# Two-layer diffusion backbone on one core: the attention projection cut into 512-column chunks and moved between layer norm, states and retention, the residual spilled to DRAM, retention without its centring and cross-decay steps

## The reference

```python
p_lat = u_lat @ w_in_l                       # u = modulated RMS norm of h
kA, vA, kB, vB, qA, qB, gF, gB, pool, glu = split(p_lat)
# A: differential attention, 4 heads, rotary on q and k
# B: retention in chunks of 128 tokens, forward and backward
scores = einsum('bhncd,bhnmd->bhncm', q, k) * dmat          # dmat = gamma ** distance
y = einsum('bhncm,bhnme->bhnce', scores, v)
cross_decay = exp(lg[:, None] * (j + 1.0))
y = y + einsum('bhncd,nbhde->bhnce', q, s_prev) * cross_decay[...]
# head layer norm: subtract the mean over a head's 64 channels, divide by the deviation
yn = (y - mu) * lax.rsqrt(var + 1e-6)
yB = silu(gF) * yn_forward + silu(gB) * yn_backward
# C: pooling windows, D: gated convolution, layer norm, silu, 256x256 product
h = h + gm * rms_norm(concat(yA, yB, yC, yD) @ w_out)
h = h + gf * rms_norm(swiglu(modulate(rms_norm(h))))
```

## Time and profile before

| | |
|---|---|
| median of three runs | 3718.29 us |
| the profiled execution | 3710.92 us, its span 3709.1 us |
| PE busy | 3221.3 us, 87% |
| DVE busy | 1846.1 us, 50% |
| ACT busy | 1045.0 us, 28% |
| mean granted TensorE clock | 0.881 |

### The profile page before, as it was taken

One profiled execution on the slowest core, in us unless ns is written; L12 is line 12 of the kernel. 1 busy time (PEld: TensorE's weight loads), 2 busy tenths in 40 slices (PEclk: granted clock), 3 DMA queues, 4 the chain that ended last, 5 costly groups with the idle time before them and its releaser, 6 DMA issues.

```text
span 3709.1 us, 45803 instructions
## 1 busy us (share of the span) xinstructions
PE 3221.3 (87%) x17774; PEld 1859.2 (50%) x17774; DVE 1846.1 (50%) x2565; ACT 1045.0 (28%) x1514; POOL 301.9 (8%) x208
## 2 busy tenths in 40 slices
PE   6798778777889999999999489679787899999997
PEld 6344544566454665555545234445666444444443
DVE  1794745788447211222225595746776364122235
ACT  2311213444344111111113311214444353111122
POOL 2400000000121000000002230000000210000001
PEclk8999669566889999999999699778666999999998
DMA  4110010011112321111111100011111222111112
GB/s 182 48 41 17 6 36 35 35 45 45 50 53 89 115 91 63 40 36 44 40 51 63 56 35 35 6 42 46 57 57 40 80 90 103 51 50 47 51 57 102
DMA packets 59451, 206.87 MB, mean 56 GB/s; under 512 B 7360, under 2 KB 8384, under 8 KB 59328
## 3 DMA queue, kind: packets, MB, share of 16 engines
q1 hardware_dynamic: 58176, 199.89, 15.1%
q10 hardware_dynamic: 1152, 5.24, 0.4%
HBM read 200.91 MB, written 4.19 MB: 55 GB/s over the span
## 4 chain that ended last, share of the span: by engine, by line
PE 54%; issue 26%; DVE 13%; ACT 5%; POOL 1%; DMA 0%; SPq 0%; POOLq 0%; DVEq 0%; ACTq 0%
PE PS L555 49%; DVE R L1578 4%; DVE wlo L1317 2%; PE PS L740 1%; ACT X L1031 1%; ACT R L1029 1%; DVE R L1395 1%; PE PS L613 1%; DVE R L1382 1%; ACT whi L984 1%; POOL st L1945 1%; PE PS L796 1%; DVE R L1700 1%; PE PS L586 1%; DVE X L1674 0%
## 5 line engine op out<-in xcount | busy, mean ns | idle before, releaser
L555 PE MATMUL PS<-R,whi 128*128 128x512 f16 (+1 forms) x7808 | 2131.5, 360 | 121.8 <-DVE wlo L1317 50.1
L555 PE MATMUL PS<-R,wlo 128*128 128x512 f16 (+1 forms) x3904 | 1404.7, 360 | 0.0
L555 PEld LDWEIGHTS PS<-R,whi 128*128 128x128 f16 x7808 | 765.8, 99 | 902.8 <-issue 68.7
L1317 DVE SCALAR_TENSOR_TENSOR wlo<-stage,whi 128x1024 f16<-128x1024 f32 (+1 forms) x260 | 332.0, 1277 | 513.5 <-ACT whi L984 495.7
L555 PEld LDWEIGHTS PS<-R,wlo 128*128 128x128 f16 x3904 | 385.2, 99 | 382.2 <-issue 17.8
L984 ACT ACTIVATE whi<-stage 128x1024 f16<-128x1024 f32 (+1 forms) x260 | 268.7, 1034 | 183.5 <-PE PS L555 133.6
L1876 POOL TENSOR_TENSOR X<-X 128x512 f32<-128x512 f32 (+2 forms) x105 | 154.6, 1475 | 1755.7 <-ACT X L1248 1611.2
L1578 DVE SCALAR_TENSOR_TENSOR R<-X,small,R 128x1024 f32<-128x1024 f32 (+1 forms) x180 | 219.1, 1267 | 1.8
L1816 DVE SCALAR_TENSOR_TENSOR X<-X,PS 128x512 f32<-128x512 f32 (+3 forms) x60 | 62.0, 1034 | 305.6 <-PE PS L555 305.5
L650 PE MATMUL PS<-ident,R 128*128 128x128 f32 x656 | 146.9, 374 | 74.1 <-DVE R L1440 46.9
L1811 DVE SCALAR_TENSOR_TENSOR X<-X,PS 128x512 f32<-128x512 f32 (+3 forms) x60 | 62.1, 1035 | 297.5 <-ACT X L1265 297.5
(11 more groups left out here) (183 smaller groups left out, 2517.6 us busy)
## 6 DMA issues: line engine op xcount, KB each, us to landing
stage<-in_w_gu SPq DMA_DIRECT2D x120, 512.0 KB, 3.4
X<-in_w_ada SPq DMA_DIRECT2D x60, 512.0 KB, 3.5
stage<-in_w_down SPq DMA_DIRECT2D x48, 512.0 KB, 3.5
stage<-in_w_in SPq DMA_DIRECT2D x44, 512.0 KB, 3.5
stage<-in_w_out SPq DMA_DIRECT2D x32, 512.0 KB, 3.5
T<-in_w_ada SPq DMA_DIRECT2D x20, 512.0 KB, 3.5
R<-in_w_ada SPq DMA_DIRECT2D x16, 512.0 KB, 10.4
stage<-in_w_down SPq DMA_DIRECT2D x16, 384.0 KB, 2.9
```

The costliest lines, as they stand in the source:

```text
L555: last = mm(slot(j, t0, t1)[:, c0 - t0:c1 - t0], w[:, j, k, :], row, start=(k == 0 and q == 0), stop=(k == K - 1 and q == 2))
L1317: STT(wlo[:, j, 0:K, :], stage[:, j, 0:K, :], WS, whi[:, j, 0:K, :], ALU.mult, ALU.subtract).then_inc(S["w_lo"], 1)
```

## The change: what it does

- **Chunks.** The six attention units are cut into chunks of one unit by one span (512 or 256 columns), 18 in layer 0 and 16 in layer 1, each with its own PSUM bank. PE runs chunk 0 ahead of the layer norm's first sums, 1 ahead of its second, 2 to 4 between the pooling products and the 256x256 product, 5 ahead of the first state step, 6 inside the state steps, 7 behind them, and one chunk behind each retention tile. ACT copies every chunk out (`a_evac`). Chunks 2, 5, 8, 11, 14, 17 of layer 0 have 256 columns; in layer 1 it is 2, 5, 12, 15.
- **Residual.** The chunks' results and the rotary tables lie in the rows of `H`. In layer 0 the residual is loaded once more from the input `x`; in layer 1 it is written to the output tensor at the layer's start and read back. The reads stand after the stacks, ahead of the ring of `w_ada`.
- **Retention.** The values' transposes become products with a matrix `centre` (identity less 1/64 in each head's block), so the head mean is zero from the start. The masks are divided by `cross` once a layer, so the output is y/cross and its scale is undone by the norm; the epsilon is scaled likewise. State part and masked part add up in PSUM. `centre` on DVE is gone; ACT squares straight from PSUM.
- **Rotary and stacks.** All permutation products, value transposes and stacks run in one loop over the 12 (layer 0) or 10 (layer 1) rotated spans, the stack two spans behind; ACT copies three of four stacks, DVE one.

```diff
+        centre = sb("centre", [P, P])
...
-        st8 = sb("st8", [P, 4, 8])
+        spare = X[:, 3 * PADW + TOK:4 * PADW]
+        st8 = spare[:, 0:32].rearrange("p (a g) -> p a g", a=4)
+        eps_z = spare[:, 32:40]
...
+        ropeA_tab = (R[:, H + 6, :], R[:, H + 7, :])
+        A_EARLY = 8
+        A_EARLY_BANKS = (3, 4, 5, 3, 4, 7, 0, 3)
+        def a_chunks(l):
+            return [(v, c0, c1, c1 == TOK) for v in range(A_UNITS)
+                    for c0, c1 in spans(first_tok(l) if v in (2, 3) else 0)]
...
# SP
                     sp.wait_ge(S["h_rows"], rows_before(4 * l + 1, 0))
+                    for d in range(KD):
+                        sp.dma_start(out[d], R[:, H + d, CTX:TOK]).then_inc(S["spilled"], 16)
...
+                if l:
+                    sp.wait_ge(S["spilled"], 16 * KD)
+                for j in range(2):
+                    sp.dma_start(ropeA_tab[j], a["ropeA"][j]).then_inc(S["a_tab"], 16)
+                sp.wait_ge(S["roped"], at("roped", l) + len(rope_chunks(l)))
+                sp.dma_start(perm[:, :], a["permA"]).then_inc(S["a_tab"], 16)
+                stream(unit0(l, "in") + ahead, NIN - ahead, KD, a["w_in"][l][ahead:NIN])
...
                 sp.wait_ge(S["yb_done"], at("yb_done", l) + NTILE - first_tok(l) // P)
-                for j in range(2):
-                    sp.dma_start(xrow(2 + j), a["ropeA"][j]).then_inc(S["a_tab"], 16)
-                sp.dma_start(SW[:, 0:704], a["stk"]).then_inc(S["a_tab"], 16)
-                sp.dma_start(perm[:, :], a["permA"]).then_inc(S["a_tab"], 16)
-                stream(unit0(l, "in") + ahead, NIN - ahead, KD, a["w_in"][l][ahead:NIN])
+                sp.dma_start(SW[:, 0:704], a["stk"]).then_inc(S["stk_tab"], 16)
                 sp.wait_ge(S["stk_ps"], at("stk_ps", l) + len(stacks(l)))
+                sp.wait_ge(S["vt_ps"], at("vt_ps", l) + NTILE)
+                for d in range(KD):
+                    if l < LAYERS - 1:
+                        sp.dma_start(R[:, H + d, :], a["x"][d]).then_inc(S["h_back"], 16)
+                    else:
+                        sp.dma_start(R[:, H + d, CTX:TOK], out[d]).then_inc(S["h_back"], 16)
...
# PE
+                def a_chunk(n):
+                    v, c0, c1, last_of_unit = a_chunks(l)[n]
+                    bank = a_bank(n)
+                    earlier = [m for m in range(n) if a_bank(m) == bank]
+                    if earlier:
+                        a_evacuated(earlier[-1])
+                    pe.wait_ge(S["w_lo"], u0 + 16 + v + 1)
+                    for k in range(KD):
+                        for q, (w, part) in enumerate(((whi, 0), (whi, 1), (wlo, 0))):
+                            last = mm(PS[:, bank, 0:c1 - c0], w[:, v % 2, k, :], hl(U + k, part, c0, c1),
+                                      start=(k == 0 and q == 0), stop=(k == KD - 1 and q == 2))
+                    last.then_inc(S["units" if last_of_unit else "a_ps"], 1)
...
-                pool_products(2, 2 * len(sp0))
+                pool_products(2, 4)
+                a_chunk(2)
+                pool_products(4, 2 * len(sp0))
+                a_chunk(3)
+                a_chunk(4)
...
# retained_out
-                        pe.wait_ge(S["y_mid"], at("y_mid", l) + n)
...
                     for h in range(HB):
                         b, q = 64 * (h % 2), h // 2
-                        mm(PS[:, 2 + 3 * (h % 2), 0:256].rearrange("p (d c) -> p d c", d=2)[:, :, q * 64:(q + 1) * 64],
-                           R[b:b + 64, G + 4 + q, t * P:(t + 1) * P],
-                           states[b:b + 64, :, t, q * 64:(q + 1) * 64], start=True, stop=True)
-                    for dr in range(2):
-                        for h in range(HB):
-                            last = mm(PS[:, 1, dr * 256 + h * 64:dr * 256 + (h + 1) * 64], pmask[:, dr, h, :],
-                                      vtok[:, t, h * 64:(h + 1) * 64], start=True, stop=True)
+                        bank = Y_BANKS[n % 2] + h % 2
+                        for dr in range(2):
+                            y = PS[:, bank, dr * P + q * 64:dr * P + (q + 1) * 64]
+                            mm(y, R[b:b + 64, G + 4 + q, t * P:(t + 1) * P], states[b:b + 64, dr, t, q * 64:(q + 1) * 64],
+                               start=True, stop=False)
+                            last = mm(y, pmask[:, dr, h, :], vtok[:, t, h * 64:(h + 1) * 64], start=False, stop=True)
...
+                    a_chunk(A_EARLY + t - tq)
...
+                NR = len(rotary(l))
+                for m in range(NR + 2):
+                    if m < NR:
+                        turned_half(m)
+                    if m < NTILE:
+                        value_turn(m)
+                    if m >= 2:
+                        stacked(m - 2)
...
# ACT
+                def a_evac(n):
...
+                    A(arow(v)[:, c0:c1], PS[:, a_bank(n), 0:c1 - c0], ACT.Copy,
+                      scale=UNS * XS).then_inc(S["slot_free" if last else "a_evac"], 1)
+                    if last and v < A_UNITS - 1:
+                        hi_part(u0 + 16 + v + 2, v % 2, KD)
...
-                    A(SW[:, 0:512], ysum[n % 2], ACT.Square).then_inc(S["y_sq"], 1)
+                    A(SW[:, 0:512].rearrange("p (x g e) -> p x g e", x=2, g=4), y_psum(n), ACT.Square).then_inc(S["y_sq"], 1)
+                    a_evac(A_EARLY + n)
...
# DVE
-                    if n < NQ:
-                        centre(n)
...
+                for m in range(NR + 2):
+                    if m < NR:
+                        rotated(m)
+                    if m < NTILE:
+                        value_lo(m)
+                    if m < NR:
+                        rotated_lo(m)
+                    if m >= 2:
+                        stack_out(m - 2)
```

More of the change, by code:

```diff
@@ L808, in tok_turn @@
                         pe.wait_ge(S["k_tok"], at("k_tok", l) + i - 1)
-                    for q, row in enumerate((G + 2, G + 3, G, G + 1)):
-                        last = nc.tensor.transpose(PS[:, (6, 3)[i % 2], q * P:(q + 1) * P], R[:, row, t * P:(t + 1) * P],
-                                                   ident[:, :])
+                    for q in range(2):
+                        mm(PS[:, (6, 3)[i % 2], q * P:(q + 1) * P], R[:, G + 2 + q, t * P:(t + 1) * P], centre[:, :],
+                           start=True, stop=True)
+                    for q in range(2, 4):
+                        last = nc.tensor.transpose(PS[:, (6, 3)[i % 2], q * P:(q + 1) * P],
+                                                   R[:, G + q - 2, t * P:(t + 1) * P], ident[:, :])
                     last.then_inc(S["tr_ps"], 1)
@@ L906, in _, with turned_half, stacked @@
-                pe.wait_ge(S["rot"], at("rot", l) + len(rotary(l)))
-                for n, (m, i, j, c0, c1) in enumerate(stacks(l)):
+                def turned_half(m):
+                    i, c0, c1 = rotary(l)[m]
+                    if m >= 2:
+                        pe.wait_ge(S["rot"], at("rot", l) + m - 1)
+                    mm(PS[:, 6 + m % 2, 0:c1 - c0], perm[:, :], arow(i)[:, c0:c1],
+                       start=True, stop=True).then_inc(S["perm_ps"], 1)
+                def stacked(m):
+                    i, c0, c1 = rotary(l)[m]
@@ L1547, in _ @@
             inverse_root(0)
+            own.link(nc.vector.reciprocal(inv_cross, cross))
+            TS(undecay, inv_cross, DK ** -0.5, None, ALU.mult)
+            STT(eps_z.rearrange("p (x g) -> p x g", x=2), inv_cross.rearrange("p (g x) -> p x g", x=2), 1e-6,
+                inv_cross.rearrange("p (g x) -> p x g", x=2), ALU.mult, ALU.mult)
+            own.link(nc.vector.tensor_copy(centre[:, :], ident[:, :]))
+            dve.wait_ge(S["small_const"], 3)
+            for b in (0, 64):
+                last = TS(centre[b:b + 64, b:b + 64], ident[b:b + 64, b:b + 64], -1.0 / 64, None, ALU.add)
+            last.then_inc(S["small_const"], 1)
             modulation(0, 0, ADA_FIRST, 3072)
```

251 lines of the change are left out of this document (148 added, 103 removed).

## The result

The changed kernel takes 3725.57 us (median of 13 runs, 3719.58 to 3727.01), the kernel before 3713.13 us (13 runs): ratio 1.0031, interval 1.0022 to 1.0040. It is slower by 0.3%, a small loss that the interval still sets apart from no change, and the forecast of 3630 us was wrong. The profiled execution has a span of 3723.8 us, 14.7 us longer than before.

The account below looks back on a forecast made before the run. PE was taken to bound only the attention projection, 198 us, to be moved into stretches where PE idles. Layer 0 less 50.6 and layer 1 less 37.4, together 88, gave 3622.9 us profiled, forecast 3630 us; range 3590 to 3675 us.

Parts of the forecast that it names:

- norm and states: Layer norm and state steps with the early chunks: 72.4 to 95 us in layer 0, 62.6 to 76.4 in layer 1.
- retention: Retention tiles, PE the bound with a chunk each, 10.4 or 7.8 us a tile: 100.0 us in layer 0, 84.4 in layer 1.
- rotary and stacks: Rotary loop of 4.0 us per 512-column span, 2.4 per 256: 47.6 us in layer 0, 42.8 in layer 1.
- stall by the reads: Layer 1's attention: residual reads queued ahead of the `w_ada` unit hold up PE's modulation product, 13 us.
- tables and projection, both: Attention projection with the tables' wait, 104.0 us in layer 0 and 94.0 in layer 1, gone as a stage.
- A: Better packing: state products at 0.13 us, tighter rotary loop, no read stall; 3590 us whole, 3605 about half; chance 0.20.
- C: Slower than before: PE at 1.2 GHz through the retention tiles, 170 us more, 3800 us; chance 0.04.
- B: Clock stays low in the new rotary loop, 28 us more, with some in the early chunks 3665 us; chance 0.17.
- D: Chunks only move and DVE's chain behind them grows as much: near the time before, 3710 us; chance 0.04.
- the sites of the chunks: Norm stage: chunks 3 and 4 in the open in layer 0, 10.4 us; chunks 2 to 4 hidden in layer 1's 13.8 us gap.

Follow-up runs that it names:

- e15: Changed kernel in its order, each state product over all 128 rows instead of one half, so retention computes something else: 3617.17 us.
- e2: Changed kernel with the same 16 products of a retention tile, eight state products first, then eight masked ones: 3612.25 us.
- e10: Changed kernel with state and masked products still alternating, but each masked product two pairs behind its state product: 3671.6 us.
- e11: Changed kernel with a tile's products in turn two state products, two masked ones: 3628.5 us.
- e12: e1 with the residual's reads placed behind the next weight ring instead of ahead of it: 3589.2 us.
- e1: Changed kernel with four state products (both directions at once) instead of eight, all ahead of a tile's eight masked products: 3599.05 us.
- e9: e1 with the residual's reads behind the next ring and layer 0's chunks 3 and 4 ahead of the last pooling products: 3582.47 us.
- e3: Changed kernel with the later chunks, their copies and low parts behind the retention loop instead of one in each tile: 3782.64 us.
- e5: Changed kernel with the later chunks behind the retention loop, as in e3, and outputs grouped as in e1: 3678.95 us.

## Why the prediction was wrong

By its steps, forecast and measured:

| step | forecast, us | measured, us |
|---|---|---|
| layer 0: norm and states | 95 | 92.3 |
| retention | 100.0 | 157.7 |
| rotary and stacks | 47.6 | 44.3 |
| layer 1: norm and states | 76.4 | 80.3 |
| retention | 84.4 | 124.6 |
| rotary and stacks | 42.8 | 39.9 |
| stall by the reads | 13 | 13.4 |
| tables and projection, both | 0 | 0 |

*Retention* is the step that failed: "a state product that stands between products over all 128 rows I price like these, 0.25", and with it the masked products beside it at 0.25, all of the tile at clock 1.00. In place of 0.25 stood 0.365 us at the upper clock and 0.617 at the lower, for both kinds: the overlap that 0.25 took for granted was missing, since the weights of each product were loaded only when it began (e15's loads start ahead). And 58% of layer 0's stage was at the lower clock. Retention misses by 98 us; the other steps miss by up to 4 us each and nearly cancel, 5 us in all. e15, which is the changed kernel with that assumption made true, ran at 3617 us, 13 us from the forecast.

The cost has two parts. e2 and the changed kernel differ in 14 changes a tile; at the upper clock each costs 0.73 less 0.36, halved: 0.18 us, so 2.6 us a tile and 26 us in layer 0's ten tiles. Their retention differs by 66 us. The other 40 us are the clock: 0.71 against 0.96, with transposes, scores and part of the chunk slow. A second way, an estimate from the stage's time and clock, gives 42 us: 58% of 157.7 us at half the clock costs 46 us, e2's one fall 4. The runs show that the clock falls in every tile with 15 changes and not with 7 or fewer in layer 0; what in the alternation makes it fall they do not show.

*The rivals.* A had the right question: a state product in a block does take 0.13 us (e2), but not where the changed kernel puts it. Its 18 us are eight state products at 0.13 instead of 0.25 us in 18 tiles, and no run shows 0.13 for one that stands between masked ones: there it is 0.365 us. The traces have 0.13 us for halves in turn (e2) and loads 0.05 us ahead for products over 128 rows in a row (e15). That the turn of the halves is what makes them cheap, as the prediction says of the scores, shows where e10 and e11 differ: e11's two state products, one over each half, take 0.37 us to the masked one (452.59 to 452.96), e10's three, of which the first two are over one half, 0.59 us (453.81 to 454.40), so the product that repeats a half adds 0.22 us. For 64 rows between 128 rows the trace of before has no price, and the one measured, 0.365 us, is dearer than both kinds in a block (0.13 and 0.23). I had used A only for a price below my 0.25, never to ask whether these two kinds are in each other's way. C was the mechanism in part: 58% of layer 0's retention at clock 0.50 and half of layer 1's, about where C's own sum uses up the gain. My ground against it, that the clock is up again soon after a stream without a gap starts, holds for the chunk (from 466.04 to 469.7 in the timeline, 3.7 us), but the clock falls again in the outputs of every tile. I should have asked what the new outputs do to the clock, and not only the chunk; the chance of 0.04 was far too low. B did not happen: the rotary loops ran at 0.96. D's result, a time near the one before, came about by another way. Two ends of the range are looser than their working: half of A's 42 us gives 3609 us, not 3605, and B with a stall dearer by 4 us 3669, not 3675. Neither decides anything here.

*Right* were the sites of the chunks: 3 and 4 in the open in layer 0 (256x256 at 398.35), hidden in layer 1 with 1.9 us to spare; the rotary loops to within 3.3 us, though PE's waits in layer 0's name ACT (9.1 us) more than DVE (2.7); no stage left for the projection; the stall of 13 us, of which e12 gives the reads 9.5 (the forecast had 10.4 for their transfer; that a small load waits behind them no row of before shows, so this step was an estimate until e1 and e12). Layer 1's norm and states came 4 us later than forecast.

*The rest.* The table's steps make up 5.2 of the 14.7 us by which the span grew: 1.0 in layer 0 and, with the stall, 4.2 in layer 1. Layer 0's stretch begins 4.4 us later than before, at 348.0, but so much also lies between kernels that are alike up to there: its first chunk starts at 343.59 in e1 and at 347.98 in e12. Layer 1's attention takes 353 us where it took 346, at clock 0.68 instead of 0.69. That does belong to the change: from the first to the last modulation product it is 290.8 us before, 297.4 in the changed kernel and 293.8 to 296.9 in e1, e9, e10, e12 and e15. The forecast had nothing for it, and no experiment was made on its cause.

## What to carry to other kernels

Do not interleave small products over 64 rows with products over 128 rows: group them by rows and let the bank's accumulation stay open. Here each change cost 0.12 us (e11) to 0.18 us (the changed kernel against e2), and the clock of layer 0's retention was 0.71 with 15 changes a tile and 0.96 with one. When a dense stream is added to a loop to use idle time of TensorE, check the time and the clock of what stands next to it too: the same chunks gave 1.00 beside e1's grouped products and 0.71 beside alternating ones. Price a new order of products by rows of that order; where the trace has none, the bound has to reach upwards too.

## What the runs showed of the hardware

A product over 128 rows that took 0.22 us beside its like was faster than one over 64 rows between products over 128 (0.365 us): doubling the rows of the state products gained 108 us in the kernel. A float32 masked product cost 0.23 us in a block and 0.16 to 0.17 us between float16 products of 512 columns. Without a chunk in its tiles, the retention loop ran at the lower clock nearly throughout however its products were ordered (0.52 in e3, 0.50 in e5 from the second tile on, 0.54 before). Between products of one height the next weights were loaded ahead of their product (0.05 to 0.22 us in e15); at a change between 64 and 128 rows the load started only with it (456.25 and 456.61 in the changed kernel).
